# Three of four parts of one modulation product move from TensorE to VectorE as running sums, beside the gating of layer 0

## The chip, the cores and the metric

The kernel runs on one core of a Trainium2 chip. The time is the device time of one execution in microseconds (us); a run's time is about 1.8 us longer than the span from its first to its last instruction that the trace shows. TensorE (PE in the rows; PEld is its weight load), VectorE (DVE), ScalarE (ACT) and GpSimd (POOL) each work through an instruction list of their own, in order, and wait for one another by semaphores. Transfers are issued by SyncE (SP, queue q1), by ScalarE (queue q10) and by GpSimd (queue q0); the three queues share the core's 16 DMA engines.

## What is computed

The reference is one inference step of two layers over 384 tokens (three tiles of 128: one of context, two of latents) of width 1024, in fp32. Cut to what matters here:

```python
def adaln_params(cond, w, b):
    m = (jax.nn.silu(cond) @ w + b)[:, None, :]
    return jnp.split(m, 6, axis=-1)      # shift1, scale1, gate1, shift2, scale2, gate2

for l in range(DEPTH):
    sh1, sc1, ga1, sh2, sc2, ga2 = adaln_params(c, mod_w[l], mod_b[l])
    h = rms_norm(x, norm1_g[l]) * (1 + sc1) + sh1
    x = x + ga1 * mixer(h)          # layer 0: short convolution || spatial gating; layer 1: Fourier || attention
    h = rms_norm(x, norm2_g[l]) * (1 + sc2) + sh2
    x = x + ga2 * hier_moe(h)       # 16 experts in 4 groups, two experts for each token
```

There are two conditions (`c_ctx` for the context, `c` for the latents), so each modulation product is a vector of 2 by 1024 times a matrix of 1024 by 6144. The kernel makes it in three pairs of vectors for each layer, called `(l, i)`: pair (1, 0) holds shift1 and scale1 of layer 1, 2048 columns.

## The kernel before

**The modulation products.** The weights of a pair come in four parts of 2 MB each: a part holds for each of the 128 partitions two rows ("chunks" c = 0, 1) of 2048 columns. PE's `mod_part(l, i, part)` (L1232) takes a part in 8 matmuls: the stationary operand is 32 columns of `cs32` (the two conditions after silu, and zeros), the moving one 512 columns of a chunk, and the sum over all parts and chunks builds up in PSUM bank 7. After the fourth part DVE's `mod_rows` (L757) adds the bias. Parts are put between other matmuls of PE by the table `between`; in the convolution of layer 0 there is one part after each group of 16 rows in the trace (8 matmuls, which the trace counts twice each).

**Layer 0's mixer on PE.** Four rounds j of the convolution, each of three groups `gate_c`, `xa`, `gate_b` (L1455) with the parts between; then the spatial gating: for four g, a `u` group (L1472) and three small matmuls (L1475); then `project_out` (L1295). PE's order in `project_out` is written by hand: output tile t and half n in turn, and between them the turning of the updated residual for the router, `turn_raw` (L1276), which for tile 0 stands after (t, n) = (1, 0) and waits for `x1` 1, the finished residual tile 0, from DVE.

**DVE beside it.** For each j the convolution's sums (L1042 to L1052), which release `y_conv`; for each g the gate (L1058, L1062), which releases `y_sgu`. PE waits for `y_sgu` g-1 before it overwrites the banks two g later, and for all four before `project_out`. In `project_out` DVE multiplies each PSUM half by the gate row and adds it to the residual (L813, L814). Its first L813 also waits for `zeroed`.

**What `zeroed` counts.** The experts' results go to a DRAM table `y_rows`, one of 768 by 1024 for each layer, which must be zero first. ACT writes both from a zero tile `nothing` (L676) when it has evacuated `sguT`; all of these writes, of both layers, must have landed before DVE's first L813.

**Loads.** SP issues loads in one fixed order; each waits for the last user of its place in a ring of 12 slots of 1 MB. After the modulation parts come the output projection's two loads (`out0.0`, `out0.1`, 2 MB each, after the last convolution group), then the first experts' weights in pairs of 1 MB: to slot 6, 10, 8 (each after the pair (1, 0) part that lies there), to slot 4 (after the `u` groups), to slot 0 (after `project_out`), and so on. POOL issues the small moves of modulation vectors through DRAM (`put_mods`, `take_columns`) and `take_rows`, four broadcasts of 512 KB in all 128 partitions, which the second norm of layer 0 uses.

Of the kernel before, what the change touches and what calls it, by code (L numbers as in the profile page):

```python
# [5 lines left out]
F32 = mybir.dt.float32  # L6
# [34 lines left out]
C_LOW = C_OVER + STEPS + 1  # L41
C_END = C_LOW + PAIRS * PAIRS


# [4 lines left out]
def program(nc, x_prompt, x_sample, cache_ckv, cache_kpe, c, c_ctx, mod_w, mod_b, norm1_g, norm2_g,  # L49
# [3 lines left out]
    with ExitStack() as ctx:  # L53
# [110 lines left out]
        shifts = scratch(7624, NG + NE)  # L164
        nothing = scratch(4608, 1536)
        yg = [pool[:, s * SLOT:s * SLOT + TILES * D] for s in (8, 4)]
# [55 lines left out]
        def mod_part(l, i, part, at):  # L222
            item(f"mod{l}.{i}.{part}", 2, mod_w[l, :, i * 2 * D:(i + 1) * 2 * D].rearrange("(p c) n -> p c n", c=DC)[:, 2 * part:2 * part + 2],
                 (2, 2 * D), ("mod_mm", 4 * (3 * l + i) + part + 1), at)

# [109 lines left out]

        N_EARLY, N_LATE = 2, 22

# [64 lines left out]
        def _(gps):  # L402
# [117 lines left out]
            put_mods(0, 2)  # L520
            take_columns(0, 2, (0,))
            put_mods(1, 0)
            take_columns(1, 0, (0, 1))
            gps.wait_ge(S("gain_rows"), 32)
            gain_rows(1)
            gps.wait_ge(S("y_sgu"), 4)
            take_rows(0)
            rows_made(0)
# [30 lines left out]
        def _(act):  # L559
# [79 lines left out]
            def constants():  # L639

                late = [(cst[:, C_CS1:], consts[:, C_CS1:])]
                late += [(convw[:, k, :].rearrange("p (h b) -> p h b", h=2), ev_conv_w[0, k].rearrange("(h p b) -> p h b", h=2, b=2)) for k in range(3)]
                late += [(sguw, ev_sgu_w[0].rearrange("g p q -> p g q")),
                         (sgub, row(ev_sgu_b[0].rearrange("g n -> (g n)"), 4 * P).rearrange("p (g n) -> p g n", g=4)),
                         (qg[:, :], od_q_norm_g[0].rearrange("(p c) -> p c", c=3)),
                         (kvg, row(od_kv_norm_g[0], KVL)), (ckv, cache_ckv[0, 0]), (kpe[:, 1, :], cache_kpe[0, 0])]
                for l in range(2):
                    late += [(wr[:, l, :, 0:NG], moe_wg[l].rearrange("(p c) g -> p c g", c=DC)),
                             (wr[:, l, :, NG:], moe_we[l].rearrange("(p c) g e -> p c (g e)", c=DC)),
                             (rb[:, l, 0:NG], row(moe_bg[l], NG)),  # L650
                             (rb[:, l, NG:], row(moe_be[l].rearrange("g e -> (g e)"), NE))]
                late += [(sgug[:, g:g + 1], ev_sgu_norm_g[0].rearrange("(g d a) -> g d a", g=4, a=1)[g]) for g in range(4)]
                assert len(late) == N_LATE
                for dst, src in late:
                    act.dma_start(dst, src).then_inc(S("late"), 16)
# [18 lines left out]
            for l in range(2):  # L674
                for part in range(4):
                    act.dma_start(y_rows[l].rearrange("(p r) d -> p (r d)", p=P)[:, 1536 * part:1536 * (part + 1)], nothing).then_inc(S("zeroed"), 16)  # L676
            router_in(0)
# [69 lines left out]
        def _(dve):  # L747
# [4 lines left out]
            def mod_rows(l, i):  # L752
# [5 lines left out]
                else:  # L758
# [3 lines left out]
                        .then_inc(S("mod_row"), 1)  # L762

            def first_columns():
                dve.wait_ge(S("mod_cmm"), 1)
# [37 lines left out]
            def project_out(l):  # L803
# [3 lines left out]
                dve.wait_ge(S("gate"), 32 * (2 * l + 1))  # L807
                dve.wait_ge(S("zeroed"), 128)
                for t in range(TILES):
# [227 lines left out]
            for j in range(4):  # L1037
# [15 lines left out]
                if j < 2:  # L1053
                    mod_rows(0, j + 1)
            mod_rows(1, 0)
            for g in range(4):
                dve.wait_ge(S("sgu_mm"), g + 1)
                link(v_.scalar_tensor_tensor(sv.rearrange("p (t n) -> p t n", t=TILES),  # L1058
# [4 lines left out]
                dve.sem_inc(S("y_sgu"), 1)  # L1063
            dve.wait_ge(S("columns10"), 64)
            scales(1)
            router_weights(0)
            project_out(0)
            router(0)
            place_tokens(0)
            experts(0)  # L1070
            experts_out(0)
            for t in (1, 2):
# [146 lines left out]
        def _(pe):  # L1219
            mm, tr = nc.tensor.matmul, nc.tensor.transpose  # L1220

            def mod_part(l, i, part):
# [7 lines left out]
                for c in range(2):  # L1230
                    for j in range(4):
                        ins = mm(ps[32 * j:32 * j + 32, 7, :], cs32[:, 2 * part + c, :], w[:, c, j * 512:(j + 1) * 512],  # L1232
                                 start=part + c == 0, stop=part + c == 4)
                ins.then_inc(S("mod_mm"), 1)

            def first_columns():
# [200 lines left out]
            for t in range(TILES):  # L1437
# [4 lines left out]
                if t == 1:  # L1442
                    mod_part(0, 1, 0)
            between = {1: (0, 1, 1), 2: (0, 1, 2), 3: (0, 1, 3), 4: (0, 2, 0), 5: (0, 2, 1), 6: (0, 2, 2), 7: (0, 2, 3),
                       8: (1, 0, 0), 9: (1, 0, 1), 10: (1, 0, 2), 11: (1, 0, 3)}
            for j in range(4):
# [20 lines left out]
            for g in range(4):  # L1467
# [6 lines left out]
                for t in range(TILES):  # L1474
                    ins = mm(ps[:, bs, t * P:(t + 1) * P], vn[:, t, g * P:(g + 1) * P], sguT[:, g, :], start=True, stop=True)  # L1475
                ins.then_inc(S("sgu_mm"), 1)
            pe.wait_ge(S("y_conv"), 4)
            pe.wait_ge(S("y_sgu"), 4)
# [179 lines left out]
def constants():  # L1658

    import numpy as np  # L1660

    out = np.zeros((P, C_END), np.float64)
    out[:, C_ID:C_ID + P] = np.eye(P)
# [26 lines left out]
    out[:, C_ONE] = 1  # L1690
    out[:, C_OVER:C_LOW] = HALF * np.arange(STEPS + 1)
    out[:, C_LOW:C_END] = np.tril(np.ones((PAIRS, PAIRS)), -1).reshape(-1)
    out[:, C_OVER] = -1
# [28 lines left out]
```

## Time and profile before

| what | value |
|---|---|
| median of 3 runs | 768.74 us (764.72 to 770.04) |
| the profiled execution: time, span | 763.69 us, 761.9 us |
| mean granted TensorE clock | 0.963 |
| busy PE, PEld, DVE, ACT, POOL | 91%, 51%, 32%, 19%, 22% of the span |
| chain that ended last | PE 75%, DMA 14%, DVE 5% |
| moved by DMA | 219.46 MB, mean 288 GB/s |

A busy share is a mean over stages with different limits. What the change is worth is decided between 125 and 226 us, from the convolution's third round to the router of layer 0, and there by which wait ends last at each of PE's waits. The granted clock is TensorE's: 1.00 is 2.4 GHz, 0.50 is 1.2 GHz.

### The profile page before, as it was taken

To read this page: it belongs to the slowest core of one execution; us is meant where nothing else is said; L and a number is where in the kernel's file an instruction comes from. 1 tells how busy PE (TensorE), PEld (TensorE's weight loads), DVE (VectorE), ACT (ScalarE), POOL (GpSimd) and SP (SyncE) were. 2 spreads that over 40 slices of the span, in tenths; PEclk is the share of its full clock that TensorE was granted. 3 is DMA by queue.
4 is the path that set the end of the run, shared out by engine and by line. 5 is a ranking of instruction groups with operands and counts; after the bars stand their busy time and mean duration, and the time that the engine had idled before them with its cause. 6 is when DMAs were issued, how large, how long until landed. Compare 5 with 4: busy or idle time off the path is not lost.

```text
span 761.9 us, 9565 instructions
## 1 busy us (share of the span) xinstructions
PE 692.9 (91%) x3667; PEld 391.0 (51%) x3667; DVE 246.5 (32%) x525; ACT 142.2 (19%) x291; POOL 165.7 (22%) x221
## 2 busy tenths in 40 slices
PE   1789999999999999999889999799799989999990
PEld 0335544464555666556445454355445556666650
DVE  0201212211236232223641324455311732323346
ACT  2101000000221122122121110455211121222201
POOL 5001011011331222313110210167214112223212
PEclk9799999999997999999989999999999899999996
DMA  9999999299539999995590494903600999879842
GB/s 331 393 360 303 393 385 394 88 405 424 227 137 399 362 422 421 420 421 236 199 406 18 184 387 138 413 2 133 212 17 28 392 391 407 350 265 419 369 153 117
DMA packets 53207, 219.46 MB, mean 288 GB/s; under 512 B 13773, under 2 KB 20941, under 8 KB 33968
## 3 DMA queue, kind: packets, MB, share of 16 engines
q1 hardware_dynamic: 31520, 178.59, 58.9%
q0 software_dynamic: 9664, 23.41, 8.3%
q10 hardware_dynamic: 11984, 16.92, 6.3%
q8 instruction: 27, 0.44, 0.2%
q14 instruction: 12, 0.10, 0.0%
HBM read 206.53 MB, written 20.68 MB: 298 GB/s over the span
## 4 chain that ended last, share of the span: by engine, by line
PE 75%; DMA 14%; DVE 5%; issue 2%; ACT 1%; SPq 1%; POOL 0%; ACTq 0%; DVEq 0%; POOLq 0%
PE ps L1381 14%; PE ps L1295 11%; PE ps L1455 8%; PE ps L1406 7%; DMA pool<-in_mod_w 6%; PE ps L1491 5%; PE ps L1232 5%; DMA pool<-in_moe_w 4%; PE ps L1472 3%; PE ps L1626 3%; PE ps L1551 2%; PE ps L1337 2%; PE ps L1285 2%; PE ps L1609 1%; PE ps L1368 1%
## 5 line engine op out<-in xcount | busy, mean ns | idle before, releaser
L1381 PE MATMUL ps<-pool 128*64 128x256 f32 x928 | 103.6, 379 | 1.1 <-issue 1.1
L1381 PEld LDWEIGHTS ps<-pool 128*64 128x64 f32 x928 | 76.5, 137 | 30.4 <-issue 8.3
L1295 PE MATMUL ps<-pool,turned 128*128 128x512 f32 x192 | 84.6, 595 | 0.0
L1232 PE MATMUL ps<-pool,cs 128*32 128x512 f32 x384 | 48.8, 636 | 20.0 <-DMA pool<-in_mod_w 11.1
L1455 PE MATMUL ps<-turned,pool 128*128 128x384 f32 x192 | 64.8, 492 | 0.0
L1295 PEld LDWEIGHTS ps<-pool,turned 128*128 128x128 f32 x192 | 35.7, 190 | 41.3 <-issue 41.1
L1406 PE MATMUL ps<-pool 128*64 128x512 f32 x240 | 54.8, 597 | 1.8 <-DMA pool<-in_moe_w 0.7
L1455 PEld LDWEIGHTS ps<-turned,pool 128*128 128x128 f32 x192 | 36.8, 196 | 30.4 <-issue 8.9
L960 DVE SCALAR_TENSOR_TENSOR pool<-ps,pool 128x256 f32<-128x256 f32 x20 | 9.7, 484 | 112.1 <-PE ps L1381 112.1
L413 POOL TENSOR_SCALAR rstd<-ss 128x1 f32<-128x1 f32 x24 | 9.5, 395 | 157.4 <-ACT xn L579 125.3
L543 POOL TENSOR_SCALAR pool<-pool 128x384 f32<-128x384 f32 (+1 forms) x30 | 30.5, 1031 | 60.4 <-DVE pool L1155 60.3
L1491 PE MATMUL ps<-pool,turned 128*128 128x512 f32 (+1 forms) x96 | 40.1, 578 | 2.6 <-DVE turned L786 2.6
L1381 PE MATMUL ps<-turned,pool 128*64 128x256 f32 x272 | 39.4, 379 | 0.0
L579 ACT ACTIVATE xn<-x 128x1024 f32<-128x1024 f32 x15 | 15.8, 1055 | 117.1 <-DVE x L814 86.1
L969 DVE TENSOR_TENSOR pool<-ps,xn 128x1024 f32<-128x1024 f32 x20 | 24.5, 1225 | 38.0 <-PE ps L1406 35.2
L1232 PEld LDWEIGHTS ps<-pool,cs 128*32 128x32 f32 x384 | 10.9, 113 | 49.5 <-issue 29.5
L423 POOL DMA_INDIRECT pool<-h_rows,of_now x18 | 29.6, 1647 | 15.0 <-POOL of_now L419 15.0
L1406 PEld LDWEIGHTS ps<-pool 128*64 128x64 f32 x240 | 18.8, 136 | 27.5 <-issue 26.5
L813 DVE TENSOR_TENSOR xn<-ps,ga 128x512 f32<-128x512 f32 x12 | 8.3, 691 | 75.6 <-PE ps L1295 61.5
L1381 PEld LDWEIGHTS ps<-turned,pool 128*64 128x64 f32 x272 | 27.5, 137 | 9.7 <-issue 2.6
L1368 PE MATMUL ps<-cst,pool 128*128 128x128 f32 x176 | 28.7, 287 | 3.9 <-DMA pool<-h_rows,of_rows 2.9
L1491 PEld LDWEIGHTS ps<-pool,turned 128*128 128x128 f32 x96 | 18.8, 199 | 23.1 <-issue 22.2
(245 smaller groups left out, 912.9 us busy)
## 6 DMA issues: line engine op xcount, KB each, us to landing
pool<-in_moe_w SPq DMA_DIRECT2D x72, 1024.0 KB, 12.3
pool<-in_mod_w SPq DMA_DIRECT2D x24, 2048.0 KB, 11.0
turned<-in_moe_w SPq DMA_DIRECT2D x18, 1024.0 KB, 13.6
pool<-in_ev_w_in SPq DMA_DIRECT2D x6, 1024.0 KB, 20.3
y_rows<-pool ACTq DMA_DIRECT2D x8, 768.0 KB, 20.4
xn<-in_moe_w SPq DMA_DIRECT2D x6, 1024.0 KB, 14.9
pool<-y_rows ACTq DMA_DIRECT2D x12, 512.0 KB, 6.3
pool<-in_ev_w_in SPq DMA_DIRECT2D x2, 2048.0 KB, 22.0
```

The costliest lines, as they stand in the source:

```text
L423: nc.gpsimd.indirect_dma_start(out=hg, out_offset=None, in_=h_rows[:, :], in_offset=bass.IndirectOffsetOnAxis(ap=index, axis=0), bounds_ch ...
L543: ins = nc.gpsimd.tensor_scalar(probs(h, t), probs(h, t), pinv[:, h % 2, t:t + 1], None, ALU.mult)
L969: v_.tensor_tensor(out, bank2(4, D), gates, ALU.mult).then_inc(S(f"L{l}_ys"), 1)
L1232: ins = mm(ps[32 * j:32 * j + 32, 7, :], cs32[:, 2 * part + c, :], w[:, c, j * 512:(j + 1) * 512], start=part + c == 0, stop=part + c == 4)
L1295: ins = mm(ps[:, 2 * t + n, :], yT[:, k, t * P:(t + 1) * P], weight(parts[k // 4], 4, D)[:, k % 4, n * 512:n * 512 + 512], start=k == 0, s ...
L1368: ins = tr(bank2(2, D)[:, cc * P:(cc + 1) * P], rows[:, cc::DC], ident)
L1381: ins = mm(ps[m, k, 0:DE], hTe.rearrange("p (c n) -> p c n", c=DC)[:, cc, m], w[e][:, cc, :], start=cc == 0, stop=cc == DC - 1)
L1406: ins = mm(ps[m, 4 + n, :], hidT[:, cc, m], w2[e][:, cc, n * 512:n * 512 + 512], start=cc == 0, stop=cc == 1)
L1455: ins = mm(ps[:, (3, 0)[j % 2] + k, 0:T], weight(f"{name}.{j // 2}", DC, 256)[:, cc, j % 2::2], hT[:, cc, :], start=cc == 0, stop=cc == DC ...
L1472: mm(ps[:, bu, 0:T], weight("u", DC, 512)[:, cc, g * P:(g + 1) * P], hT[:, cc, :], start=cc == 0, stop=cc == DC - 1)
L1491: ins = mm(ps[:, b, 0:hi - lo], hT[:, cc, t * P:(t + 1) * P], w[:, k, lo:hi], start=cc == 0, stop=cc == DC - 1)
L1626: ins = mm(scores(h, t), qT[0:QH, h % 2, t * P:(t + 1) * P], kT[0:QH, h % 2, 0:P] if t == 0 else kT[0:QH, h % 2, P:512], start=True, stop= ...
```

## The change

Of pair (1, 0) PE keeps part 0. Parts 1 to 3 are made on DVE by `mod_products`: each chunk is multiplied by the condition's value of that partition and added to a running sum of 128 by 2048, one for each condition (`mod_sums`; the first in `xn`, the second in three pieces of 1024, 512 and 512). The first chunk of part 1 sets the sums (a TENSOR_SCALAR), the five others add to them (SCALAR_TENSOR_TENSOR). Part 1 is taken between the third and the fourth convolution round; the four chunks of parts 2 and 3 one ahead of each gate. `mod_total` on PE then sums over the partitions: 8 matmuls with a one-column selector (`picks`, 64 more constants) onto what part 0 left in bank 7.

The places of the parts in the ring are now released by DVE (`mod_mac`), so the experts' first loads wait for that. The zero tile shrinks from 1536 to 1024 columns to make room for sums, so `y_rows` is written in 12 pieces instead of 8. DVE's `mod_rows(1, 0)` moves behind the gates, `scales(1)` behind the experts of layer 0, and on POOL `take_rows(0)` moves ahead of `put_mods(1, 0)`.

```diff
-        nothing = scratch(4608, 1536)
+        nothing = scratch(4608, 1024)
+        picks = scratch(6656, 64)
+        mod_sums = [[xn[:, 0:2, :].rearrange("p a b -> p (a b)")], [xn[:, 2, :], scratch(6144, 512), scratch(5632, 512)]]
...
-                 (2, 2 * D), ("mod_mm", 4 * (3 * l + i) + part + 1), at)
+                 (2, 2 * D), ("mod_mac", part) if (l, i) == (1, 0) and part else ("mod_mm", 4 * (3 * l + i) + part + 1), at)
...
+            gps.wait_ge(S("y_sgu"), 4)
+            take_rows(0)
             put_mods(1, 0)
             take_columns(1, 0, (0, 1))
             gps.wait_ge(S("gain_rows"), 32)
             gain_rows(1)
-            gps.wait_ge(S("y_sgu"), 4)
-            take_rows(0)
             rows_made(0)
...
-                for part in range(4):
-                    act.dma_start(y_rows[l].rearrange("(p r) d -> p (r d)", p=P)[:, 1536 * part:1536 * (part + 1)], nothing).then_inc(S("zeroed"), 16)
+                for part in range(6):
+                    act.dma_start(y_rows[l].rearrange("(p r) d -> p (r d)", p=P)[:, 1024 * part:1024 * (part + 1)], nothing).then_inc(S("zeroed"), 16)
...
+            def mod_products(part, chunks):
+
+                arrived(dve, f"mod1.0.{part}")
+                w = weight(f"mod1.0.{part}", 2, 2 * D)
+                for c in chunks:
+                    for r in range(2):
+                        factor, at = cs32[:, 2 * part + c, r:r + 1], 0
+                        for piece in mod_sums[r]:
+                            n = piece.shape[-1]
+                            if (part, c) == (1, 0):
+                                ins = v_.tensor_scalar(piece, w[:, c, at:at + n], factor, None, ALU.mult)
+                            else:
+                                ins = v_.scalar_tensor_tensor(piece, w[:, c, at:at + n], factor, piece, ALU.mult, ALU.add)
+                            at += n
+                    link(ins)
+                if 1 in chunks:
+                    dve.sem_inc(S("mod_mac"), 1)
...
-                dve.wait_ge(S("zeroed"), 128)
+                dve.wait_ge(S("zeroed"), 192)
...
-            mod_rows(1, 0)
+                if j == 2:
+                    dve.wait_ge(S("cs32"), 1)
+                    dve.wait_ge(S("norm_tr"), TILES)
+                    mod_products(1, (0, 1))
             for g in range(4):
+                mod_products(2 + g // 2, (g % 2,))
                 dve.wait_ge(S("sgu_mm"), g + 1)
...
-            dve.wait_ge(S("columns10"), 64)
-            scales(1)
+            mod_rows(1, 0)
...
+            def mod_total():
+
+                pe.wait_ge(S("mod_mac"), 3)
+                for r in range(2):
+                    pieces = [p[:, at:at + 512] for p in mod_sums[r] for at in range(0, p.shape[-1], 512)]
+                    for j in range(4):
+                        ins = mm(ps[32 * j:32 * j + 32, 7, :], picks[:, 32 * r:32 * r + 32], pieces[j],
+                                 start=False, stop=r == 1)
+                ins.then_inc(S("mod_mm"), 3)
...
-            between = {1: (0, 1, 1), 2: (0, 1, 2), 3: (0, 1, 3), 4: (0, 2, 0), 5: (0, 2, 1), 6: (0, 2, 2), 7: (0, 2, 3),
-                       8: (1, 0, 0), 9: (1, 0, 1), 10: (1, 0, 2), 11: (1, 0, 3)}
+            between = {1: (0, 1, 1), 2: (0, 1, 2), 3: (0, 1, 3), 4: (0, 2, 0), 5: (0, 2, 1), 6: (0, 2, 2), 7: (0, 2, 3), 8: (1, 0, 0)}
...
+            mod_total()
             pe.wait_ge(S("y_conv"), 4)
             pe.wait_ge(S("y_sgu"), 4)
```

How the lists of instructions move shows at three places. The first is DVE, from the fourth convolution round's last sum to the end of the second gate (L1052 and L1074 write `yT` of the convolution, L1058 and L1084 are the gate; `cs` is the condition, `slot` semaphores are loads that have landed). Before:

```order
L1052 TENSOR_TENSOR turned<-pool,ps 128x384 [waits conv_mm,dve_chain]
L757 TENSOR_TENSOR mrow<-ps,mrow 128x512 [waits mod_mm]
L1058 SCALAR_TENSOR_TENSOR pool<-ps,sgug,pool 128x384 [waits sgu_mm]
L1062 TENSOR_TENSOR turned<-pool,ps 128x384 [waits dve_chain]
L1058 SCALAR_TENSOR_TENSOR pool<-ps,sgug,pool 128x384 [waits dve_chain,sgu_mm]
L1062 TENSOR_TENSOR turned<-pool,ps 128x384 [waits dve_chain]
```

And changed:

```order
L1074 TENSOR_TENSOR turned<-pool,ps 128x384 [waits conv_mm,dve_chain]
L780 SCALAR_TENSOR_TENSOR xn<-pool,cs,xn 128x2048 [waits slot10]
L780 SCALAR_TENSOR_TENSOR xn<-pool,cs,xn 128x1024
L780 SCALAR_TENSOR_TENSOR pool<-pool,cs 128x512 x2
L1084 SCALAR_TENSOR_TENSOR pool<-ps,sgug,pool 128x384 [waits sgu_mm,dve_chain]
L1088 TENSOR_TENSOR turned<-pool,ps 128x384 [waits dve_chain]
L780 SCALAR_TENSOR_TENSOR xn<-pool,cs,xn 128x2048 [waits dve_chain,slot10]
L780 SCALAR_TENSOR_TENSOR xn<-pool,cs,xn 128x1024
L780 SCALAR_TENSOR_TENSOR pool<-pool,cs 128x512 x2
L1084 SCALAR_TENSOR_TENSOR pool<-ps,sgug,pool 128x384 [waits dve_chain,sgu_mm]
L1088 TENSOR_TENSOR turned<-pool,ps 128x384 [waits dve_chain]
```

Each gate now has a chunk of four instructions ahead of it on the same engine.

The second is PE from the last group of the gating to the first turning of the residual in `project_out` (L1261 and L1298 are its first small matmuls, L1295 and L1332 the projection, L1276 and L1313 `turn_raw`). Before:

```order
L1475 MATMUL ps<-pool 128x128 [waits sguT]
L1475 MATMUL ps<-pool 128x128 x2
L1261 MATMUL ps<-wr,modcol 2x20 [waits slot2,slot0,columns01,y_sgu,y_conv]
L1261 MATMUL ps<-wr,modcol 2x20 x7
L1295 MATMUL ps<-pool,turned 128x512 x8
L1268 MATMUL ps<-pool,cst 128x20 [waits rbias]
L1268 MATMUL ps<-pool,cst 128x20
L1295 MATMUL ps<-pool,turned 128x512 x16
L1276 MATMUL ps<-cst,x 128x128 [waits x1,rbias]
```

And changed:

```order
L1511 MATMUL ps<-pool 128x128 [waits sguT]
L1511 MATMUL ps<-pool 128x128 x2
L1269 MATMUL ps<-xn,pool 32x512 [waits mod_mac]
L1269 MATMUL ps<-xn,pool 32x512 x5
L1269 MATMUL ps<-pool 32x512 x2
L1298 MATMUL ps<-wr,modcol 2x20 [waits slot2,slot0,columns01,y_sgu,y_conv]
L1298 MATMUL ps<-wr,modcol 2x20 x7
L1332 MATMUL ps<-pool,turned 128x512 x8
L1305 MATMUL ps<-pool,cst 128x20 [waits rbias]
L1305 MATMUL ps<-pool,cst 128x20
L1332 MATMUL ps<-pool,turned 128x512 x16
L1313 MATMUL ps<-cst,x 128x128 [waits x1,rbias]
```

The sum over the partitions stands between the gating and the projection; behind it nothing has moved, and `turn_raw` still waits for `x1`.

The third is ACT's list at the zero writes, from the evacuation of `sguT` to the squares of residual tile 0. Before:

```order
L672 ACTIVATE pool<-ps 128x512 [waits sgu_tr]
L676 DMA y_rows<-pool 128x1536 [waits nothing]
L676 DMA y_rows<-pool 128x1536 x7
L579 ACTIVATE xn,ss<-x 128x1024 [waits x1]
```

And changed:

```order
L676 ACTIVATE pool<-ps 128x512 [waits sgu_tr]
L680 DMA y_rows<-pool 128x1024 [waits nothing]
L680 DMA y_rows<-pool 128x1024 x11
L583 ACTIVATE xn,ss<-x 128x1024 [waits x1]
```

The same bytes are written in rows of 4 KB instead of 6 KB for each partition, half as many rows again.

## Rows read from the trace of the kernel before

**Rows 1.** Chain of waits, 140 to 200: start us, us, what.

```profile
146.79 1.85 PE ps L1232 x16
...
149.23 5.16 PE ps L1472 x16
154.39 0.67 PE ps L1475 x6
...
172.55 1.40 issue
...
182.12 13.93 PE ps L1295 x32
196.05 0.89 PE ps L1276 x8
```

**Rows 2.** Stretches: length, busy PE, PEld, DVE, ACT, POOL, PEclk, DMA share, GB/s.

```profile
226.00:246.00 20.00, 19.22 (x59) 10.97 (x60) 13.74 (x61) 2.90 (x5) 1.68 (x3) 0.69 0.99 398
246.00:299.00 53.00, 52.28 (x400) 34.61 (x398) 16.02 (x21) 10.98 (x17) 13.59 (x17) 1.00 0.98 400
```

**Rows 3.** Timeline of DVE, 125 to 157: start us, us, instruction, idle before it.

```profile
125.23 0.56 DVE L1052 TENSOR_TENSOR turned<-pool,ps 128x384 f32<-128x384 f32 x1 [1.14 <-PE ps L1455]
...
155.10 0.62 DVE L1058 SCALAR_TENSOR_TENSOR pool<-ps,sgug,pool 128x384 f32<-128x384 f32 x1 [5.70 <-PE ps L1475]
155.75 0.55 DVE L1062 TENSOR_TENSOR turned<-pool,ps 128x384 f32<-128x384 f32 x1
```

**Rows 4.** Groups of instructions by form, DVE: busy us, mean ns, idle before.

```profile
L965 DVE SCALAR_TENSOR_TENSOR xn<-ga,pool 128x1024 f32<-128x1024 f32 x20 | 25.5, 1276 | 0.0
...
L778 DVE TENSOR_SCALAR xn<-x,rstd 128x1024 f32<-128x1024 f32 x6 | 4.5, 750 | 18.5 <-POOL rstd L414 18.5
...
L1049 DVE SCALAR_TENSOR_TENSOR pool<-pool,convw 128x255 f32<-128x255 f32 x4 | 1.9, 484 | 0.1
```

**Rows 5.** Timeline of SP's queue, 112 to 119: load of part 1.

```profile
112.60 0.37 SPq L365 DMA_DIRECT2D pool<-in_mod_w  x1
```

**Rows 6.** Transfers by issue, 60 to 260: size of each, median us to landing.

```profile
pool<-in_mod_w SPq DMA_DIRECT2D x11, 2048.0 KB, 9.5
```

**Rows 7.** Timeline of DVE, 188 to 192: the first residual tile.

```profile
188.81 0.69 DVE L813 TENSOR_TENSOR xn<-ps,ga 128x512 f32<-128x512 f32 x1 [14.10 <-DMA y_rows<-pool]
...
190.97 0.69 DVE L814 TENSOR_TENSOR x<-x,xn 128x512 f32<-128x512 f32 x1
```

**Rows 8.** Timeline of SP's and ACT's queues, 146 to 154: output weights, zero writes.

```profile
146.82 0.88 SPq L365 DMA_DIRECT2D pool<-in_ev_w_out  x2
...
149.27 4.41 ACTq L676 DMA_DIRECT2D y_rows<-pool  x8
```

**Rows 9.** Queues, 130 to 220, ACT's: packets, MB, share of 16 engines.

```profile
q10 hardware_dynamic: 1152, 6.29, 16.8%
```

**Rows 10.** Queues, 153 to 154, ACT's (its first packets).

```profile
q10 hardware_dynamic: 8, 0.05, 11.8%
```

**Rows 11.** Queues, 157 to 161 (SP moves rows of 4 KB).

```profile
q10 hardware_dynamic: 180, 0.93, 56.2%
q1 hardware_dynamic: 180, 0.74, 44.7%
```

**Rows 12.** Queues, 169 to 173, ACT's (SP moves rows of 8 KB).

```profile
q10 hardware_dynamic: 136, 0.74, 44.5%
```

**Rows 13.** Queues, 177 to 178, POOL's (its first packet of `take_rows`).

```profile
q0 software_dynamic: 1, 0.00, 1.0%
```

**Rows 14.** Queues, 181 to 185, ACT's (three queues at work).

```profile
q10 hardware_dynamic: 98, 0.58, 34.8%
```

**Rows 15.** Stretch 384 to 386, columns as in the second group.

```profile
384.00:386.00 2.00, 1.58 (x2) 0.84 (x3) 1.97 (x3) 0.47 (x2) 1.35 (x2) 0.50 0.96 411
```

**Rows 16.** Timeline of PE from 366: layer 1's first projection, with idle before.

```profile
384.42 8.58 PE L1491 MATMUL ps<-pool,turned 128*128 128x512 f32 x16 [2.60 <-DVE turned L786]
```

**Rows 17.** Chain of waits, from 395: a later group of the same matmuls.

```profile
395.73 6.42 PE ps L1491 x16
```

More of the change, by code:

```diff
@@ L42 @@
 C_END = C_LOW + PAIRS * PAIRS
+C_PICK = C_END
+C_DRAM = C_PICK + 64
 def cond_of(tile):
@@ L334, in router_out @@
             return ps[:, (7, 6, 0)[t], 0:NG + NE]
-        N_EARLY, N_LATE = 2, 22
+        N_EARLY, N_LATE = 2, 23
         def row(src, n):
@@ L639, in constants @@
             def constants():
-                late = [(cst[:, C_CS1:], consts[:, C_CS1:])]
+                late = [(cst[:, C_CS1:], consts[:, C_CS1:C_END]), (picks, consts[:, C_PICK:])]
                 late += [(convw[:, k, :].rearrange("p (h b) -> p h b", h=2), ev_conv_w[0, k].rearrange("(h p b) -> p h b", h=2, b=2)) for k in range(3)]
@@ L1070, in _ @@
             experts(0)
+            dve.wait_ge(S("columns10"), 64)
+            scales(1)
             experts_out(0)
@@ L1660, in constants @@
     import numpy as np
-    out = np.zeros((P, C_END), np.float64)
+    out = np.zeros((P, C_DRAM), np.float64)
     out[:, C_ID:C_ID + P] = np.eye(P)
@@ L1691, in constants @@
     out[:, C_OVER:C_LOW] = HALF * np.arange(STEPS + 1)
+    for r in range(2):
+        out[:, C_PICK + 32 * r + r] = 1
     out[:, C_LOW:C_END] = np.tril(np.ones((PAIRS, PAIRS)), -1).reshape(-1)
@@ L1715 @@
     arrays["in_consts"] = constants()
-    args.append(nc.dram_tensor("in_consts", (P, C_END), F32, kind="ExternalInput").ap())
+    args.append(nc.dram_tensor("in_consts", (P, C_DRAM), F32, kind="ExternalInput").ap())
     for i, shape in enumerate(OUTS):
```

## Prediction

> **What bounds the kernel now.** I read the chain of waits first. From 146.79 to 226 it runs over PE almost without a gap [rows 1]: the last modulation part of 1.85, four gating groups of 5.16 + 0.67, 1.40 of waiting for the last gate, then `project_out`. So work taken from PE ahead of 173.95 (172.55 + 1.40) brings `project_out` forward. Next the table of stretches: between 246 and 299 PE is busy for 52.28 of 53 us and the DMA engines for 0.98 of the time [rows 2]; the loads that fill this stage are started by PE's own events (SP's first late load waits for the end of `project_out`). A shift of `project_out` therefore passes through the experts and to the end at its full size, forward or back. Last, DVE's timeline around `project_out`: its first L813 waited 14.10 us for the zero writes to `y_rows`, until 188.81 [rows 7]. This cost nothing, since PE asks for tile 0 only at 196.05 [rows 1] and DVE has it at 190.97 + 0.69 = 191.66 [rows 7], 4.4 before that. These 4.4 us of slack are the number to watch: the change brings PE's request forward and alters the writes.
>
> **PE.** Three parts go: 3 x 1.85 = 5.55 [rows 1]. The last convolution group then ends at 146.79 + 1.85 - 5.55 = 143.1, and the gating's last matmuls at 172.55 - 5.55 = 167.0. `mod_total` adds 8 matmuls of the shape of a part, 1.85.
>
> **DVE.** A chunk for both conditions is 2048 + 1024 + 512 + 512 columns. The nearest rows with two tensors and a scalar are 1276 ns for 1024 columns and 484 for 255 [rows 4], so 1.03 ns a column; that gives 2.33, 1.28, 0.75 and 0.75, together 5.1 if nothing overlaps, and 4.6 if each new one started 0.15 early; I take 5.0. The first chunk has one tensor only (750 ns for 1024, [rows 4]) and lies between 3.0 and 5.1. Part 1 has landed by 112.60 + 9.5 = 122.1 [rows 5, 6], and DVE is free at 125.8 [rows 3], so part 1 is done between 133.8 and 136. The fourth round's sums can't start before PE's second group of that round, a group of over 5 us ahead of 143.1, about 137.8: part 1 lies in DVE's idle time. From 143.8 on the chunks are ahead of the gates. The first gate's matmuls end at 155.06 - 5.55 = 149.5, after its chunk (148.8), and the gate takes 1.2 [rows 3], to 150.7. Then chunk and gate, 6.2, are more than PE's 5.83, and DVE leads: the last chunk ends at 150.7 + 6.2 + 6.2 + 5.0 = 168.1, the last gate at 169.3. PE waits 1.1 for the chunk, sums for 1.85 and starts `project_out` at 170.0, **3.95 earlier**. With chunks of 4.6 it would be 4.9 earlier, with 5.1 3.7.
>
> **The zero writes.** This is the term that I think decides. PE reaches `turn_raw` of tile 0 at 196.05 - 3.95 = 192.1. DVE needs 2.85 from the release to the finished tile [rows 7], so the zeros must have landed by 189.2 to cost nothing; at 193.2 the whole gain is gone.
>
> What the writes get of the DMA engines is seen in the queues. In 4 us in which SP moved 4 KB rows, ACT's and SP's queue had 180 packets each, though ACT's rows are of 6 KB and took more of the bytes [rows 11]: two queues with work take turns by packets, not by bytes. So the writes' time goes by their number of rows. It was 1152 with the small closing ones (8 x 144; [rows 9]) and becomes 12 x 144 = 1728, at the same bytes.
>
> By turns per us: 180/4 = 45 against 4 KB rows [rows 11], 136/4 = 34 against 8 KB rows [rows 12], 98/4 = 24.5 with POOL's `take_rows` as a third queue [rows 14]. First the run of before, as a test. The writes start at 153.5 [rows 10]. `out0.0` has some 2 us left (75 turns, to 155.7); `out0.1` has 4 x 128 + 32 = 544 packets (12.1 us, to 167.8); experts' rows of 8 KB until POOL joins at 177.7 [rows 13] (337 turns); the remaining 196 at 24.5 take to 185.7. DVE was released at 188.81, 3.1 later; I carry the 3.1 over.
>
> Now the changed plan. With 4 KB rows a turn is shorter: by bytes in one turn of all queues (10.2 to 8.2 KB, 14.3 to 12.3, 18.4 to 16.4) the rates become 56, 39.5 and 27.5. SP issues `out0` at 143.1 instead of 146.82 [rows 8], the writes are issued 5.55 earlier at 143.7, and their first packets come between 145.5 (the delay that SP's had) and 147.9 (4.2 after the issue, as before); I take 146.7. `out0.0` then has more left, by my estimate 190 turns (it runs alone 3 us less; to 151.5), `out0.1` 544 (to 161.2), experts' rows until `take_rows`, released 4.5 earlier, joins at 173.2 (474); the remaining 520 at 27.5 take 18.9, to 192.1, and with 3.1 the release is at **195.2**. SP's queue doesn't run dry: slot 6 is free at 136, slot 10 at 155.7, slot 8 at 168.1. The bounds of the start give 193.6 and 197.0; the sum of all bytes that are then in flight, 21.0 MB at (0.93 + 0.74)/4 us [rows 11] from 145, ends at 195.3 + 3.1 = 198.4, which nothing exceeds.
>
> Tile 0 is then finished at 198.05, and PE, idle from 192.1, turns it **2.0 later** than before (0.4 to 3.8).
>
> A page bears on the turns. The Trainium skill (DMA: Bandwidth & Descriptors, Queues, rings and completion order) has each engine drain a packet of typically 9 to 17 descriptors from one ring before it goes to the next. By that, a zero write's 9 on an engine would trade against up to 17 of `out0.1`, the writes would get about half as many turns there, and tile 0 would be later by up to 3.2, the bound just given. The 180 to 180 speak against it, and the sum goes by them.
>
> **The clock.** PE would be idle for some 6 us. In layer 1 a stretch of light work and waits of this kind left the granted clock at 0.50 (1.2 GHz) between 384 and 386 [rows 15], and the first group after it took 8.58 [rows 16] where a later one of the same shape took 6.42 [rows 17]: **2.2 lost**. Below, it costs nothing (the clock may hold); above, see the third rival. I take 2.2, as the idle time is of that length.
>
> **Priced at nothing.** The constants' load grows by 32 KB in ACT's list; it is waited for before the first convolution sums, which PE needs only two rounds later. `scales(1)` is tiny and now stands in DVE's wait for the experts' rows. `mod_rows(1, 0)` waits for `mod_total` and delays DVE by a PSUM add; PE first needs what follows after the first projection group. On POOL `put_mods(1, 0)` now queues behind the 2 MB of `take_rows`, so POOL comes to its first root at about 199, when ACT's squares of tile 0 (ready with tile 0 at 198) need it: even, with nothing behind it until tile 1. Without the stall it would be a few us late, and the next tile's wait absorbs that.
>
> **Sum.** -3.95 is buried by the stall: +2.0 + 2.2 = +4.2, so 763.69 + 4.2 = 767.9 in the profiled execution. That execution is 5.05 below the median of 768.74; the four executions shown (763.69, 764.72, 768.74, 770.04) have their middle at 766.7, 3.0 above it. I forecast 767.9 + 3.0 = **770.9**.
>
> **Rivals.**
> - *The zeros land in time* (before 189.2), because their queue starts at once and gets more turns than counted. For: the first packets' delay is known to 2.4 us only. Against: it takes 6 us less than the count, which met the run of before within 3.1. Then all 3.95 stay: 759.7 + 3.0 = 762.8. Chance 0.17.
> - *A short stall*: zeros at 190 to 194, no loss of clock. -3.1 to +0.8, in the middle 765.5. Chance 0.23.
> - *The clock stays low*. After the light work of the router the granted clock was 0.69 in the mean over 20 us, 226 to 246 [rows 2], so 0.50 for some 12. If the stall brings that on in `project_out`, where PE is full, about 6 us go instead of 2.2, and with a late release (+3.8) it is +10: 776.7, slower than before. It decides when the granted clock after the stall is 0.50 for over 10 us. Chance 0.10.
> - *Turns by blocks of rows.* If an engine took several rows of `out0.1` for each of the zeros', the release would come as late as the sum of bytes allows, 198.4, and tile 0 5.2 later than before; with the clock +7.4, 774.1. Against: 180 to 180 [rows 11]. Chance 0.03. This is the rule of the Trainium skill cited above (DMA: Bandwidth & Descriptors).
> - The forecast, a stall of 5 to 8 us and a short loss of clock: 0.47, by itself 767 to 774.
>
> **Range and chances.** From the first rival to just short of the third: 762 to 776. A difference of 1% (7.7 us) is about what a measurement of this kernel tells from no change. Faster by that could only come from the scatter of runs, 0.04; slower needs the third rival or a late release with scatter, 0.11; within, 0.85.
>
> **What would show it.** PE's chain: no parts between the fourth round's groups, a sum of 1.85 at about 168, `project_out` at 170. DVE: chunks of 5.0. ACT's queue: 1728 packets, 39 a us against 8 KB rows. The wait of DVE's first projection product ends at about 195 on the zero writes, and PE's `turn_raw` waits for it for some 6 us, then the granted clock falls. If PE goes through there without a wait, the count of turns was wrong; if it stands at `mod_total` for several us, the price of the chunks was.

## The result, and the profile after

The changed kernel takes 770.88 us (median of 20 runs, 765.43 to 778.29) against 765.04 for the kernel before, run beside it (20 runs): a ratio of 1.0073, 95% interval 1.0053 to 1.0092. 770.9 was forecast. Within the 1% that the prediction counts as no change, it is slightly slower by the interval, 5.8 us by the medians. Ratios leave out runs over 1.5% above the fastest of their kernel (one here, two of seven in experiment 1); medians are over all runs. The profiled execution took 771.8 us (span 770.0, granted clock 0.958).

The chain of waits after, from 150 to 218 (start us, us, what). In [rows 1] the chain ran over PE but for 1.40:

```profile
150.73 2.67 ACTq L680
153.42 42.60 DMA y_rows<-pool
196.11 0.70 DVE xn L835
...
198.27 0.70 DVE x L836
198.97 0.14 issue
199.11 1.95 PE ps L1313 x8
201.05 8.51 PE ps L1332 x16
...
211.26 6.96 PE ps L1332 x16
```

The 42.60 of zero writes now stand on the path, and PE's first groups behind them (1.95 and 8.51) are longer than the same shapes were or later are (0.89 in [rows 1], 6.96 here).

PE's timeline after, 166 to 210, with the idle time before a group and what ended it:

```profile
166.42 0.83 PE L1511 MATMUL ps<-pool 128*128 128x128 f32 x6
168.86 1.48 PE L1269 MATMUL ps<-xn,pool 128*32 128x512 f32 x10 [1.61 <-DVEq L784]
...
170.60 0.56 PE L1298 MATMUL ps<-wr,modcol 128*2 128x20 f32 x16
171.09 7.13 PE L1332 MATMUL ps<-pool,turned 128*128 128x512 f32 x16
...
199.11 1.95 PE L1313 MATMUL ps<-cst,x 128*128 128x128 f32 x8 [6.41 <-DVE x L836]
200.84 8.72 PE L1332 MATMUL ps<-pool,turned 128*128 128x512 f32 x16
```

Two waits: 1.61 for the last chunk of the sums, 6.41 for residual tile 0. DVE's timeline after shows where both come from:

```profile
163.17 0.55 DVE L1088 TENSOR_TENSOR turned<-pool,ps 128x384 f32<-128x384 f32 x1
163.88 3.55 DVE L780 SCALAR_TENSOR_TENSOR xn<-pool,cs,xn 128x2048 f32<-128x2048 f32 x2 [0.15 <-DVE turned L1088]
167.34 1.41 DVE L780 SCALAR_TENSOR_TENSOR pool<-pool,cs 128x512 f32<-128x512 f32 x2
168.90 0.62 DVE L1084 SCALAR_TENSOR_TENSOR pool<-ps,sgug,pool 128x384 f32<-128x384 f32 x1 [0.15 <-DVE pool L780]
...
196.11 0.69 DVE L835 TENSOR_TENSOR xn<-ps,ga 128x512 f32<-128x512 f32 x1 [24.02 <-DMA y_rows<-pool]
```

A chunk takes 4.87 (163.88 to 168.75), and DVE hardly pauses between chunks and gates. The first projection product waits until 196.11 for the writes; in [rows 7] that was 188.81.

The queues after: packets, MB, share of 16 engines. From 130 to 220, ACT's ([rows 9] had 1152 for the same bytes), and from 148 to 149, its first:

```profile
q10 hardware_dynamic: 1728, 6.29, 17.1%
```

```profile
q10 hardware_dynamic: 16, 0.07, 16.0%
```

From 157 to 161, beside the 4 KB rows of `out0.1` on SP's queue, from 166 to 170, beside 8 KB rows, and from 180 to 184, with POOL's as a third:

```profile
q1 hardware_dynamic: 221, 0.91, 54.9%
q10 hardware_dynamic: 224, 0.79, 48.1%
```

```profile
q1 hardware_dynamic: 148, 1.09, 64.6%
q10 hardware_dynamic: 155, 0.57, 35.2%
```

```profile
q1 hardware_dynamic: 113, 0.80, 47.5%
q10 hardware_dynamic: 114, 0.45, 27.6%
q0 software_dynamic: 112, 0.44, 26.9%
```

Nearly equal counts, also for rows of unequal size: 56, 38.8 and 28.5 turns a us, where 56, 39.5 and 27.5 were worked out. The Trainium skill (DMA: Bandwidth & Descriptors, Queues, rings and completion order) has an engine drain a packet of typically 9 to 17 descriptors from one ring before it turns to the next. The 113, 114 and 112 records can't tell such packets from single rows: each of these transfers has 128 rows, 8 for each of the 16 engines, so packets of 8 rows would alternate as evenly. `out0.1` has 512 rows, 32 for each engine, and the 221 to 224 beside it show no advantage for its queue.

The stretches after, with the columns of [rows 2] (the seventh number is the granted clock):

```profile
194.00:196.00 2.00, 0.00 (x0) 0.00 (x0) 0.00 (x0) 0.00 (x0) 0.00 (x0) 1.00 0.92 377
196.00:198.00 2.00, 0.00 (x0) 0.00 (x0) 1.85 (x4) 0.00 (x0) 1.66 (x3) 0.85 0.06 14
198.00:200.00 2.00, 0.89 (x5) 0.92 (x6) 1.93 (x4) 1.00 (x2) 1.65 (x4) 0.50 0.11 8
200.00:202.00 2.00, 2.00 (x7) 1.49 (x7) 0.29 (x1) 1.06 (x3) 0.74 (x2) 0.50 0.02 2
202.00:204.00 2.00, 2.00 (x3) 0.71 (x3) 0.00 (x0) 1.15 (x2) 0.77 (x1) 0.50 0.00 0
204.00:206.00 2.00, 2.00 (x6) 0.79 (x5) 0.00 (x0) 0.00 (x0) 1.92 (x2) 0.94 0.00 0
```

PE has no matmul from 192.70 (178.70 + 14.00) to 199.11. The granted clock falls between 196 and 198, is at its lower level (0.50, 1.2 GHz) until 204 and back at 1.00 from 206 on; PE works at the lower level from 199.11 to a little after 204.

Where the time went, between the two profiled executions (after minus before, from PE's timelines):

| PE reaches | before | after | difference |
|---|---|---|---|
| the start of `project_out` | 173.95 | 170.60 | -3.35 |
| `turn_raw` of tile 0 (195.89 here, 196.05 in the chain of before) | 195.89 | 199.11 | +3.22 |
| the end of the last router product (L1285, now L1322) | 226.03 | 231.28 | +5.25 |
| the first expert | 245.65 | 249.03 | +3.38 |
| the end of the span | 761.9 | 770.0 | +8.1 |

The first three lines are the change, up to the scatter of where an execution starts its gating (1.6 between the kernel before and the control below). What the other two add is scatter, as the control shows.

### The profile page after: what moved, and what is told of

The parts are those of the page before. It is cut to its first block, busy times and chain, and to the rows that moved or that the text cites. A ratio compares the mean times of both kernels' runs of the same rounds, so it can differ in the third digit from the quotient of the medians.

```text
span 770.0 us, 9536 instructions
## 1 busy us (share of the span) xinstructions
PE 690.8 (90%) x3635; PEld 391.9 (51%) x3635; DVE 273.0 (35%) x549; ACT 142.1 (18%) x291; POOL 164.5 (21%) x221
## 4 chain that ended last, share of the span: by engine, by line
PE 63%; DMA 23%; DVE 7%; issue 2%; ACT 1%; ACTq 1%; SPq 1%; POOL 0%; POOLq 0%; DVEq 0%
PE ps L1418 13%; DMA pool<-in_mod_w 9%; PE ps L1332 8%; PE ps L1443 7%; DMA y_rows<-pool 6%; PE ps L1491 6%; PE ps L1528 5%; DMA pool<-h_rows,of_now 5%; PE ps L1259 4%; PE ps L1663 3%; PE ps L1588 2%; DMA pool<-h_rows,of_rows 2%; PE ps L1405 2%; PE ps L1374 2%; PE ps L1322 2%
## 5 line engine op out<-in xcount | busy, mean ns | idle before, releaser
L1332 PE MATMUL ps<-pool,turned 128*128 128x512 f32 x192 | 86.3, 605 | 0.0
L1259 PE MATMUL ps<-pool,cs 128*32 128x512 f32 x336 | 43.0, 641 | 20.9 <-DMA pool<-in_mod_w 12.1
L1332 PEld LDWEIGHTS ps<-pool,turned 128*128 128x128 f32 x192 | 36.4, 194 | 42.4 <-issue 42.2
L1443 PE MATMUL ps<-pool 128*64 128x512 f32 x240 | 56.4, 611 | 1.0
L417 POOL TENSOR_SCALAR rstd<-ss 128x1 f32<-128x1 f32 x24 | 9.6, 398 | 147.9 <-ACT xn L583 113.7
L1405 PEld LDWEIGHTS ps<-cst,pool 128*128 128x128 f32 x176 | 23.6, 195 | 16.4 <-DMA pool<-h_rows,of_rows 6.2
```

What stands on the lines that cost most here:

```text
L1332: ins = mm(ps[:, 2 * t + n, :], yT[:, k, t * P:(t + 1) * P], weight(parts[k // 4], 4, D)[:, k % 4, n * 512:n * 512 + 512], start=k == 0, s ...
L1405: ins = tr(bank2(2, D)[:, cc * P:(cc + 1) * P], rows[:, cc::DC], ident)
L1443: ins = mm(ps[m, 4 + n, :], hidT[:, cc, m], w2[e][:, cc, n * 512:n * 512 + 512], start=cc == 0, stop=cc == 1)
```

## The experiments

The kernel before, run beside the first four, had a median of 765.34 (24 runs), beside the last four 764.69 (34 runs).

**1. The split wait.** DVE's first product waits for layer 0's six writes alone; layer 1's are waited for ahead of the first router logits.

```diff
-                    act.dma_start(y_rows[l].rearrange("(p r) d -> p (r d)", p=P)[:, 1024 * part:1024 * (part + 1)], nothing).then_inc(S("zeroed"), 16)
+                    act.dma_start(y_rows[l].rearrange("(p r) d -> p (r d)", p=P)[:, 1024 * part:1024 * (part + 1)], nothing).then_inc(S(f"zeroed{l}"), 16)
...
-                dve.wait_ge(S("zeroed"), 192)
+                dve.wait_ge(S("zeroed0"), 96)
...
                     if t:
+                        dve.wait_ge(S("zeroed1"), 96)
                         logits(l, t - 1)
```

> The changed kernel, but DVE's first projection product waits only for the six zero writes of layer 0; those of layer 1 are waited for before the first router logits, 10 us later. Theory 1 (turns by rows: the 1728 packets of the zero writes land too late): layer 0's 864 packets have landed by about 168, so no wait at the first product, PE turns tile 0 at about 192.7 (before: 196.05, changed: 199.11), the granted clock stays 1.00 from 192 to 206, and the time is 3.4 us below before (-2 to -4.5), some 9 us below the changed kernel. Theory 2 (the loss comes from what DVE took over, from the later release of the experts' loads or from POOL's new order): another wait takes the place and the time stays 4 to 7 us above before.

Measured: 759.84 (7 runs), ratio 0.9911 (0.9873 to 0.9949). The ratio rests on five runs; the mean of all seven is 761.4, 0.995 of the kernel before's 765.4. DVE's first product waits for PE, and PE's `turn_raw` for nothing (DVE's and PE's timelines):

```profile
177.24 0.69 DVE L835 TENSOR_TENSOR xn<-ps,ga 128x512 f32<-128x512 f32 x1 [6.28 <-PE ps L1333]
```

```profile
191.41 1.04 PE L1314 MATMUL ps<-cst,x 128*128 128x128 f32 x8
192.29 7.03 PE L1333 MATMUL ps<-pool,turned 128*128 128x512 f32 x16
```

The same 1728 rows are written at the same time; only the wait is gone. So the loss of the changed kernel is this wait.

**2. The rows alone.** The kernel before, with nothing changed but the zero tile: 1024 columns, 12 writes of 4 KB rows.

```diff
-        nothing = scratch(4608, 1536)
+        nothing = scratch(4608, 1024)
...
-                for part in range(4):
-                    act.dma_start(y_rows[l].rearrange("(p r) d -> p (r d)", p=P)[:, 1536 * part:1536 * (part + 1)], nothing).then_inc(S("zeroed"), 16)
+                for part in range(6):
+                    act.dma_start(y_rows[l].rearrange("(p r) d -> p (r d)", p=P)[:, 1024 * part:1024 * (part + 1)], nothing).then_inc(S("zeroed"), 16)
...
-                dve.wait_ge(S("zeroed"), 128)
+                dve.wait_ge(S("zeroed"), 192)
```

> The kernel before, with nothing changed but the zero writes: 12 of 4 KB rows instead of 8 of 6 KB rows. Theory 1: by the count of turns the release comes at about 200 instead of 188.81 (not later than all bytes in flight, 201), PE waits some 7 us at the turning of tile 0 and loses clock: 8 to 11 us slower than before. Theory 2, or shares by bytes: release at 188 to 190, no wait of PE, within 1 us of before.

Measured: 775.59 (6 runs), ratio 1.0159 (1.0116 to 1.0202). DVE's timeline, then PE's:

```profile
201.18 0.69 DVE L813 TENSOR_TENSOR xn<-ps,ga 128x512 f32<-128x512 f32 x1 [26.56 <-DMA y_rows<-pool]
```

```profile
204.18 1.95 PE L1276 MATMUL ps<-cst,x 128*128 128x128 f32 x8 [8.22 <-DVE x L814]
205.91 7.61 PE L1295 MATMUL ps<-pool,turned 128*128 128x512 f32 x16
```

The same 6.29 MB, issued at the same point and beside the same loads, land 12.37 later (201.18 against 188.81 in [rows 7]) when they are half as many rows again. A sharing by bytes would have left the release where it was. The edit also makes twelve writes of eight; that rows take the turns, and not writes, is read from the counts above. PE waited 8.22 of the 12.37: the other 4.15 were slack, worked out as 4.4 in the prediction. Without any of the new products on DVE, the smaller tile costs more here than the whole change does.

**3. A busy wait.** The changed kernel, with seven matmuls of 512 columns into an unused bank on PE just ahead of its wait for tile 0. The stall stays, the idleness goes.

```diff
+                            if l == 0:
+                                keep_clock(7, *[512] * 7)
```

> The changed kernel with 7 matmuls of 512 columns (about 6 us, results unused) on PE in front of its wait for the first residual tile. Theory 1 with the clock term: the tile still comes at 199, but the granted clock is 1.00 from 196 to 206 instead of 0.50, so PE is some 2.5 us earlier at 210 than in the changed kernel (209.4 becomes about 206.9); in the whole, 1 to 3 us less than the changed kernel. If the idle clock is not a cost: same as the changed kernel.

Measured: 768.54 (12 runs), ratio 1.0042 (1.0015 to 1.0070), 2.3 under the changed kernel by the medians; the intervals of the two ratios overlap, so the gain is read from the profile. PE's timeline, and one stretch:

```profile
193.20 6.17 PE L1353 MATMUL ps<-cst 128*128 128x512 f32 x14
200.30 1.13 PE L1313 MATMUL ps<-cst,x 128*128 128x128 f32 x8 [0.94 <-DVE x L836]
201.27 7.03 PE L1332 MATMUL ps<-pool,turned 128*128 128x512 f32 x16
```

```profile
202.00:204.00 2.00, 2.00 (x6) 0.91 (x5) 0.00 (x0) 1.53 (x2) 0.65 (x2) 1.00 0.04 8
```

The clock stays at 1.00, and the two groups take 1.13 and 7.03 instead of 1.95 and 8.72: 2.5 us are the price of the lower clock. From `turn_raw` to the last router product it is 29.73 instead of 32.17. The late release itself remains: `turn_raw` still comes at 200.30.

**4. The writes early.** The changed kernel, with the twelve writes ahead of ACT's wait for the gating weights.

```diff
-            act.wait_ge(S("sgu_tr"), 1)
-            a_.activation(sguT, ps[:, 6, :].rearrange("p (g n) -> p g n", g=4), ACT.Copy).then_inc(S("sguT"), 1)
             act.wait_ge(S("nothing"), 1)
...
+            act.wait_ge(S("sgu_tr"), 1)
+            a_.activation(sguT, ps[:, 6, :].rearrange("p (g n) -> p g n", g=4), ACT.Copy).then_inc(S("sguT"), 1)
```

> The changed kernel with the twelve zero writes issued on ACT ahead of its wait for the turned gating weights, about 11 us earlier, into a stretch where the DMA engines were nearly idle. Theory 1: they land by about 152, DVE's first product has no wait, PE turns tile 0 at about 192.7: 3.4 us below before (-2 to -4.5). Theory 2: the time stays 4 to 7 us above before.

Measured: 762.6 (12 runs), ratio 0.9973 (0.9943 to 1.0003). The writes are issued from 131.99 on, and PE goes through:

```profile
191.32 1.05 PE L1313 MATMUL ps<-cst,x 128*128 128x128 f32 x8
```

A second way to remove the stall without touching the rows or DVE's sums, and it gives most of the same. Against the split wait it is 2.8 more by the medians, but the intervals overlap.

**5. The control.** The kernel before with the split wait.

```diff
-                    act.dma_start(y_rows[l].rearrange("(p r) d -> p (r d)", p=P)[:, 1536 * part:1536 * (part + 1)], nothing).then_inc(S("zeroed"), 16)
+                    act.dma_start(y_rows[l].rearrange("(p r) d -> p (r d)", p=P)[:, 1536 * part:1536 * (part + 1)], nothing).then_inc(S(f"zeroed{l}"), 16)
...
-                dve.wait_ge(S("zeroed"), 128)
+                dve.wait_ge(S("zeroed0"), 64)
...
                     if t:
+                        dve.wait_ge(S("zeroed1"), 64)
```

> Control: the kernel before, with VectorE's first projection product waiting for layer 0's zero writes alone. Theory (the wait cost nothing before the change: TensorE asks for tile 0 4.4 us after it is there): within 2 us of the kernel before, so the gain of the split wait in the changed kernel is the stall's and not something else's. Rival (VectorE's earlier start in the projection is worth something in itself, for instance through earlier PSUM banks or POOL's and ScalarE's earlier norm work): 3 us or more faster than before.

Measured: 765.36 (12 runs), ratio 0.9995 (0.9972 to 1.0018): nothing. DVE's wait is gone here too, and PE had no use for it. So what the split wait gains in the changed kernel is the stall's, and the wait had slack (experiment 2 measures it). PE's timeline of this control also shows how far two executions of equal work lie apart:

```profile
175.54 0.56 PE L1262 MATMUL ps<-wr,modcol 128*2 128x20 f32 x16 [1.40 <-issue]
...
244.44 7.13 PE L1382 MATMUL ps<-pool 128*64 128x256 f32 x64 [0.24 <-issue]
254.68 0.71 PE L1369 MATMUL ps<-cst,pool 128*128 128x128 f32 x4 [3.11 <-DMA pool<-h_rows,of_rows]
```

Its `project_out` starts 1.6 later than in the profile of before, its experts 1.2 earlier, and it waits 3.11 for the experts' first gather, where the profile of before (its PE timeline) has no wait and the changed kernel one of 3.94:

```profile
245.65 7.13 PE L1381 MATMUL ps<-pool 128*64 128x256 f32 x64 [0.24 <-issue]
252.70 0.71 PE L1368 MATMUL ps<-cst,pool 128*128 128x128 f32 x4
```

```profile
249.03 7.13 PE L1418 MATMUL ps<-pool 128*64 128x256 f32 x64 [0.25 <-issue]
260.10 1.12 PE L1405 MATMUL ps<-cst,pool 128*128 128x128 f32 x4 [3.94 <-DMA pool<-h_rows,of_rows]
```

From the first expert to the end of the span it is 516.25 in the profile of before (761.9 - 245.65), 520.97 in the changed kernel's and 519.66 in the control's. In all ten profiled executions it lies between 519.5 and 521.9, but for that one. Likewise from the last router product to the first expert: 16.1 to 19.6 in all ten, 16.3 in the control and 19.6 in the kernel before, which do not differ there. So of the +8.1 between the profiles the 4.7 behind the first expert belong to a fortunate profile of before, not to the change.

**6. One chunk moved.** With the split wait, one of the four chunks goes into DVE's idle time ahead of the fourth convolution round.

```diff
                     mod_products(1, (0, 1))
+                    mod_products(2, (0,))
             for g in range(4):
-                mod_products(2 + g // 2, (g % 2,))
+                if g < 3:
+                    mod_products(*((2, (1,)), (3, (0,)), (3, (1,)))[g])
```

> The split wait for the zero writes, and one chunk (row 0 of part 2, both conditions) moved from the gates into VectorE's idle time ahead of the fourth convolution round; three chunks stay ahead of the gates. Theory (TensorE's wait of 1.61 us ahead of the sum over partitions comes from chunk plus gate, 6.2 us, against 5.83 for a gating group): that wait goes, the sum starts 1.1 to 1.6 earlier, the projection at 168.0 to 168.4 instead of 169.5, and the median is 1 to 1.6 us under the kernel with the split wait alone, so 6.5 to 8.5 under the kernel before. Rival (the wait is the last gate's own latency, the gating bounded by PE and ACT): the wait stays at 1.4 or so and the time is that of the split wait alone, within 0.5. Second rival (the earlier projection meets the zeros again): layer 0's writes end after 189 and TensorE waits for tile 0.

Measured: 760.55 (12 runs), ratio 0.9944 (0.9915 to 0.9973). PE's wait for the sums is gone:

```profile
166.55 0.83 PE L1514 MATMUL ps<-pool 128*128 128x128 f32 x6
167.31 1.48 PE L1272 MATMUL ps<-xn,pool 128*32 128x512 f32 x10
```

From the first gating group to the projection it is 25.65 (143.90 to 169.55) where it was 27.33 (143.76 to 171.09 in the changed kernel, the same 27.33 with the split wait alone). So the mechanism holds, and 1.68 is its size. The time doesn't show it: the medians of this kernel, the split wait alone and the next lie within 0.8 us of one another, and their intervals overlap.

**7. The same move with early writes.**

> As the run of the same chunk move with the split wait, but with the twelve zero writes issued ahead of ScalarE's wait for the turned gating weights' input (and one count for both layers). Theory: 1 to 1.6 us under the kernel with early writes alone, so 3.5 to 5 under the kernel before, and above the split variant by what layer 1's writes take from the loads in that stage. Rival: the early writes delay the output weights, and the projection starts no earlier than with early writes alone.

Measured: 760.29 (12 runs), ratio 0.9928 (0.9894 to 0.9961). From the first gating group to the projection again 25.64. The early writes kept nothing of that back. By the medians it is 2.3 under the early writes alone (experiment 4), with overlapping intervals.

**8. POOL's order.** With the split wait, `take_rows` goes back behind `put_mods(1, 0)`.

```diff
-            gps.wait_ge(S("y_sgu"), 4)
-            take_rows(0)
             put_mods(1, 0)
...
             gain_rows(1)
+            gps.wait_ge(S("y_sgu"), 4)
+            take_rows(0)
```

> The split wait, with POOL's old order (the moves of pair (1, 0) and the gains ahead of the four broadcasts). It tests what was priced at nothing: POOL comes 22.8 us late out of its wait for the modulation vectors, and ScalarE waits 6.1 us for POOL's first root. Theory: TensorE waits for none of it, so within 1.5 us of the split wait alone. Rival A: POOL's lateness delays the router's logits, and the old order is faster by 2 us or more. Rival B: the broadcasts start later behind the wait for the sum, take DMA time in the router's stage, and the old order is slower by 2 us or more.

Measured: 761.21 (12 runs), ratio 0.9949 (0.9924 to 0.9974), 1.4 above the split wait by the medians; the intervals overlap, so the times alone don't exclude the 2 us of rival B. In the split kernel POOL comes late out of its wait for the vectors of pair (1, 0), and ACT waits for POOL's root (POOL's timeline, then ACT's):

```profile
195.41 2.20 POOL L482 DMA_DIRECT2D modcol<-mods  x4 [22.81 <-DMA mods<-mrow]
...
198.79 0.18 POOL L417 TENSOR_SCALAR rstd<-ss 128x1 f32<-128x1 f32 x1
```

```profile
199.65 1.15 ACT L612 ACTIVATE xn<-x,rstd 128x1024 f32<-128x1024 f32 x1 [6.13 <-POOL rstd L418]
```

With the old order the root is ready at 188.16 + 0.56 = 188.72, 10.9 earlier than the 199.06 + 0.56 of the split kernel, and POOL then waits 8.73 for the broadcasts instead. Neither reaches PE: its waits for another engine in the router are the same in both profiles but for some tenths. (Its last router product took 3.60 at the lower clock, where the split kernel's took 1.96; the control's took 3.01.)

## Why the prediction was right

The chain came out as forecast; the number did too, in part by luck. The steps can be checked one at a time.

- *PE and DVE-led gating.* Right in kind. A chunk took 4.87 (5.0 taken); PE waited 1.61 for the last chunk (1.1 forecast) and summed for 1.74, 168.86 to 170.60 (1.85 taken). `project_out` was forecast 3.95 earlier and came 3.35 earlier. From the first gating group to the projection it is 27.33 instead of the 25.38 of the control (150.65 to 176.03), so of the 5.55 taken from PE 3.60 are left, whatever the start of an execution scatters. (The 4.9 given for chunks of 4.6 adds up to 5.1: PE's 167.0 and 1.85. Nothing rests on it.)
- *The zero writes.* The step that decides, the sharing by rows, was right. 1728 rows, turns by rows at 56, 38.8 and 28.5 a us against 56, 39.5 and 27.5. The release came at 196.11 (195.2 forecast, bounds 193.6 to 197.0), and the tile stall was 6.41 (about 6). But the working counts too many rows at its start: the first came after 148, outside its bounds (145.5 to 147.9), and only 108 had gone by 152 and 1119 by 174, where it has about 218 and 1230. The last go after 194, not by 192.1. The 3.1 carried over from the run of before, for which the working names no cause, covers this; that it had the right size here is luck, and without it the stall would have been forecast at about 3. That the rows and not the bytes set the time was inferred from one pair of counts [rows 11]; experiment 2 shows it.
- *The clock.* 2.2 was forecast from layer 1's stall. Against the same groups at full clock in experiment 3, `turn_raw` lost 0.82 and the projection group 1.69, together 2.5.
- *The sum.* +4.2 was forecast, from -3.95 + 5.95 + 2.2. The stage itself gave +5.25 (table above): -3.35, 6.57 longer from the projection to `turn_raw` (28.02 for 21.45), 2.03 longer from there to the last router product. With 3.60 for 3.35, free of the start's scatter, it is 5.0. The medians differ by 5.84.
- *The base.* The 3.0 put on top for the median was too much: with 20 runs and more, the kernel before lies at 764.7 to 765.3 and not at 766.7. An effect 1 to 1.6 too small and a base 1.7 too high cancelled, so 770.9 hits more closely than its terms do.
- *Priced at nothing.* The POOL order cost PE nothing in the traces (experiment 8). The moved `mod_rows` and `scales` left no wait on PE in the profile; they weren't tried alone.
- *The rivals.* The zeros did not land in time, the clock was back at 1.00 from 206 on and did not stay low into `project_out`'s rest, and blocks of rows would have put the release at 198.4. The rival that the zeros land in time priced the change without its stall at 762.8; with the stall removed and all four chunks left ahead of the gates it is 759.8, 762.6 and 761.2 (experiments 1, 4 and 8), around that price less the 1.7 of the base (761.1).

## What to carry to other kernels

A wait that costs nothing has a slack; write it down before bringing the waiter forward, because the gain ends where the slack does. Where several queues are busy, count the rows of a transfer and not only its bytes: a buffer cut by a third to make room made the writes land 12 us later at the same bytes. And one semaphore for two things holds up the early need until the late one is met: counting the two layers apart turned a loss of 0.7% into a gain, 0.9% by the five runs of experiment 1 and 0.5% by the twelve of experiment 8. The 3.60 us left of PE's work are 0.5%.

## What was not expected of the hardware

- Profiles differ in places where nothing was changed: the experts' first gather took 4.7 us in the profile of before and 8.9 in the control's, and the granted clock in the router stayed at 0.50 from 226 to 238 in the one and from 226 to 232 in the other. A profile's difference of 4 us far behind the edit is no evidence.
- ACT's issue of twelve writes took 11.70 us where eight took 4.41 [rows 8]: in the chain of waits mostly about 0.5 each up to 149.06, then 1.64 and 2.67. The rows went on landing at the turns shown above, so nothing here says that it cost time.
